# RWKV scan of a hybrid trunk: products laid straight or crossed over the array, value and key parts taken ahead

## The reference

```
def step(state, inp):
    r_t, w_t, k_t, v_t, kk_t, a_t = inp
    sa = jnp.einsum("bhvk,bhk->bhv", state, -kk_t)
    state = (state * w_t[:, :, None, :] + sa[..., None] * (kk_t * a_t)[:, :, None, :]
             + v_t[..., None] * k_t[:, :, None, :])
    return state, jnp.einsum("bhvk,bhk->bhv", state, r_t)
```

## Time and profile before

| what | us |
|---|---|
| median of three runs | 3495.32 |
| profiled execution | 3495.7 |
| its span | 3493.9 |
| span from 478.2 to 1190.0: scan of layer 0 | 711.8 |
| span from 2224.4 to 2930.5: scan of layer 1 | 706.1 |
| TensorE busy in these two | 697.72 and 694.95 |
| VectorE busy | 191.41 and 191.40 |
| ScalarE busy | 228.00 and 227.82 |
| GpSimd busy | 241.34 and 241.53 |

### The profile page before, as it was taken

How to read it: one execution, slowest core, us unless ns; L and a number is a source line. 1 busy time by engine, 2 the same in 40 slices (tenths; PEclk the granted TensorE clock), 3 DMA queues, 4 the chain that set the end, 5 groups by cost and what they waited for, 6 DMA issues and landing times. The chain is left out here.

```text
span 3493.9 us, 64355 instructions
## 1 busy us (share of the span) xinstructions
PE 3155.2 (90%) x24596; PEld 2315.9 (66%) x24596; DVE 1483.0 (42%) x2280; ACT 1145.7 (33%) x2332; POOL 961.4 (28%) x880
## 2 busy tenths in 40 slices
PE   6979979999999799959969799799999997999599
PEld 4768857777777544447747688577777775444477
DVE  4127722222222367567441277222222223675674
ACT  4004422333333245433240044223333333354332
POOL 4101011244343323332241010112444443233322
PEclk9989989999999879979989899899999998799699
DMA  3224532333333200077332245323333332000763
GB/s 125 73 74 146 165 88 80 96 101 107 104 105 106 81 25 28 6 210 214 117 119 73 76 144 165 91 82 98 101 105 107 107 103 75 25 28 6 214 211 116
DMA packets 408876, 357.82 MB, mean 102 GB/s; under 512 B 102792, under 2 KB 345992, under 8 KB 408584
## 3 DMA queue, kind: packets, MB, share of 16 engines
q1 hardware_dynamic: 339656, 312.93, 29.2%
q10 hardware_dynamic: 68928, 40.93, 4.3%
HBM read 222.97 MB, written 130.84 MB: 101 GB/s over the span
## 5 line engine op out<-in xcount | busy, mean ns | idle before, releaser
L124 PE MATMUL rs_acc<-h_hi,rs_w_hi 128*128 128x512 f32 x1024 | 425.4, 415 | 0.0
L128 PE MATMUL rs_acc<-h_lo,rs_w_hi 128*128 128x512 f32 x1024 | 415.5, 406 | 0.0
L130 PE MATMUL rs_acc<-h_hi,rs_w_lo 128*128 128x512 f32 x1024 | 412.0, 402 | 0.0
L124 PE MATMUL rp_acc<-h_hi,rp_w_hi 128*128 128x512 f32 x512 | 206.1, 402 | 40.9 <-PEq L121 40.9
L1466 ACT ACTIVATE fx_prob<-fx_ST 128x512 f32<-128x512 f32 (+3 forms) x320 | 157.8, 531 | 230.7 <-PE fx_ST L1328 123.3
L1752 PE MATMUL so_acc<-so_wo_hi,so_m_hi 128*128 128x512 f32 x512 | 210.2, 411 | 25.5 <-POOL so_m_lo L1674 21.4
L124 PEld LDWEIGHTS rs_acc<-h_hi,rs_w_hi 128*128 128x128 f32 x1024 | 192.1, 188 | 53.4 <-issue 16.5
L130 PEld LDWEIGHTS rs_acc<-h_hi,rs_w_lo 128*128 128x128 f32 x1024 | 192.5, 188 | 41.4
L128 PEld LDWEIGHTS rs_acc<-h_lo,rs_w_hi 128*128 128x128 f32 x1024 | 192.6, 188 | 35.6
L124 PE MATMUL pj_acc<-h_hi,pj_w_hi 128*128 128x512 f32 (+1 forms) x512 | 207.1, 404 | 5.2 <-PEq L121 5.2
L128 PE MATMUL rp_acc<-h_lo,rp_w_hi 128*128 128x512 f32 x512 | 208.0, 406 | 0.0
(11 more groups left out here) (257 smaller groups left out, 6496.0 us busy)
## 6 DMA issues: line engine op xcount, KB each, us to landing
projT<-rs_stage SPq DMA_DIRECT2D x128, 256.0 KB, 2.3
pj_xb<-x SPq DMA_DIRECT2D x32, 512.0 KB, 3.4
projT<-rp_stage SPq DMA_DIRECT2D x64, 256.0 KB, 3.1
rs_raw<-w_in ACTq DMA_DIRECT2D x32, 512.0 KB, 4.5
rs_nat<-rw SPq DMA_DIRECT2D x128, 128.0 KB, 2.4
so_stage<-x SPq DMA_DIRECT2D x64, 256.0 KB, 3.1
rp_pre<-projT SPq DMA_DIRECT2D x16, 899.5 KB, 7.5
projT<-pj_stage SPq DMA_DIRECT2D x56, 256.0 KB, 2.0
```

The lines of the kernel that those rows point to most:

```text
L124: ins = M(acc, self.w_hi[q][:, k, 0:m], self.h_hi[:, k, cols], start=(k == 0), stop=False)
L128: M(acc, self.w_hi[q][:, k, 0:m], self.h_lo[:, k, cols], start=False, stop=False)
L130: ins = M(acc, self.w_lo[q][:, k, 0:m], self.h_hi[:, k, cols], start=False, stop=(k == KC - 1))
```

## The change

Each product goes through `product`. For odd heads either its input or its output is crossed: chunk 0 of the head lies in partitions 64 to 127 and chunk 1 in 0 to 63. A straight input with a crossed output (or the reverse) makes the products of two neighbouring heads use the four quarters of the array; even heads write to one bank, odd heads to the next. s5 goes from straight to straight. The inputs of a tile are partly loaded crossed (`later`). N, b and k are formed in one group p1, with another copy of N by `beside`. Additions of the identity or of an earlier term that VectorE made become products with the identity (`unity`, `plus`). For both chunks the parts of the state step with wz and with vm are issued ahead of g; only the part with S stays in c0 and c1. SCAN_FILL is dealt out anew. norm_sum(t,3) goes from behind the filler of g to behind that of s9, `square(t, 3)` on ScalarE from behind wz into s8, and the wait for the factor of (t,3) from c1 to ahead of the products taken ahead. The units' sums go to `bk[:, 3, 256:512]`. The forget gates' steps come later on every engine. The core of the diff:

```diff
-SCAN_FILL = (("tok", 7), ("p2", 5), ("s3", 5), ("s4", 4), ("s5", 5), ("s6", 5), ("s7", 6), ("s8", 5), ("s9", 6), ("wz", 6), ("g", 8), ("c0", 10), ("c1", 22), ("y", 2))
+SCAN_FILL = (("p1", 5), ("p2", 6), ("s3", 5), ("s4", 5), ("s5", 5), ("s6", 5), ("s7", 5), ("s8", 5), ("s9", 5), ("wz", 6), ("g", 7), ("c0", 9), ("c1", 24), ("y", 4))
...
+        def pair(k, a, n=1):
+            return bk[:, 2 * k:2 * k + 2, :].rearrange("p e (i c) -> p i e c", i=2)[:, :, :, 64 * a:64 * (a + n)]
...
-                if i == 2:
+                if i == 3:
...
-                for n, buf, slot in ((0, cr[e], (0, 3)), (1, cr[e], (1, 2)), (2, bt, None), (3, kt, None)):
+                for n, buf in ((0, cr[e][:, :, 0, :]), (1, cr[e][:, :, 1, :]), (2, bt[:]), (3, kt[:])):
                     for c in two:
                         src = rw[n * GW:(n + 1) * GW, bass.ds(t * 128 + 64 * c, 64)].rearrange("(h c) t -> c h t", c=64)
-                        sp.dma_start(buf[half[c]] if slot is None else buf[half[c], :, slot[c], :], src).then_inc(i_in[e], 16)
-                for j, n in enumerate((0, 2, 3, 4)):
-                    sp.dma_start(nat[:, j], rw[n * GW:(n + 1) * GW, bass.ds(t * 128, 128)].rearrange("(k p) t -> p k t", p=128)).then_inc(i_in[e], 16)
+                        sp.dma_start(buf[half[c]], src).then_inc(i_in[e], 16)
+                sp.dma_start(nat[:, 0], rw[0:GW, bass.ds(t * 128, 128)].rearrange("(k p) t -> p k t", p=128)).then_inc(i_in[e], 16)
+                later = nat[:, 1:4].rearrange("p j k t -> p (j k) t")
+                src = rw[2 * GW:5 * GW, bass.ds(t * 128, 128)].rearrange("(n e c) t -> e c n t", e=2, c=64)
+                sp.dma_start(later[half[0]], src[0]).then_inc(i_in[e], 16)
+                for c in two:
+                    sp.dma_start(later[half[1], :, 64 * (1 - c):64 * (1 - c) + 64], src[1][:, :, 64 * c:64 * c + 64]).then_inc(i_in[e], 16)
...
                 gates_biased(t)
-                gates_log(t)
                 for i in range(4):
-                    if i == 1:
-                        gates_low(t)
                     if i == 1 and t + 1 < NT:
                         J.pool_weights(pool, (t + 1) % 2)
+                    if i == 2:
+                        gates_log(t)
                     if (t, i) in unit:
                         scale(unit[t, i])
+                gates_low(t)
...
-            def pairs(out, left, right):
-                for h in range(NH):
-                    for c in two:
-                        ins = M(out(h, c), left(h, c), right(h, c), start=True, stop=True)
+            def at(h, c, crossed):
+                return half[c ^ (h & 1) if crossed else c]
+            def out(k, a, n, h, p):
+                return bk[p, 2 * k + h % 2, 256 * (h // 2) + 64 * a:256 * (h // 2) + 64 * (a + n)]
+            def beside(p, h):
+                return bk[p, 2, 256 * (h // 2) + 128 + 64 * (h % 2):256 * (h // 2) + 192 + 64 * (h % 2)]
+            def some(i):
+                return [(2 * i + e, u) for e in two for u in two]
+            def product(k, a, n, left, right, crossed, to, plus=None):
+                for i in two:
+                    for h, c in some(i):
+                        p = at(h, c, crossed)
+                        ins = M(out(k, a, n, h, at(h, c, to)), left(p, h), right(p, h), start=True, stop=plus is None)
+                    if plus is not None:
+                        for h, c in some(i):
+                            p = at(h, c, crossed)
+                            ins = M(out(k, a + n - 1, 1, h, at(h, c, to)), eye[p], plus(p, h), start=False, stop=True)
                 return ins
-            def of(buf, *at):
-                return lambda h, c: buf[(half[c], h) + at]
-            def slots(buf, a, n=1, b=None):
-                b = a if b is None else b
-                return lambda h, c: buf[half[c], h, (a, b)[c]:(a, b)[c] + n, :] if n > 1 else buf[half[c], h, (a, b)[c], :]
-            E1, E2 = DE[:, 1], DE[:, 2]
+            def of(buf, a=None, n=1):
+                if a is None:
+                    return lambda p, h: buf[p, h, :]
+                return lambda p, h: buf[p, h, a, :] if n == 1 else buf[p, h, a:a + n, :]
+            def unity(p, h):
+                return eye[p]
+            straight, crossed = False, True
...
                 take(pe, i_in[e], 192)
-                pairs(of(bank(0)), slots(cr[e], 0, b=3), of(bt)).then_inc(s["n_rdy"], 1)
-                pairs(of(wide(1)), of(bt), slots(cr[e], 0, 2, b=2)).then_inc(s["mb"], 1)
-                pairs(of(wide(2)), of(kt), slots(cr[e], 0, 2, b=2)).then_inc(s["mk"], 1)
-                take(pe, s["y_ev"])
                 for j in range(4):
                     for p in two:
-                        ins = Tr(bk[:, 3 + j // 2, (2 * (j % 2) + p) * 128:(2 * (j % 2) + p + 1) * 128], nat[:, j, p, :], ident[:])
+                        ins = Tr(bk[:, 4 + j // 2, (2 * (j % 2) + p) * 128:(2 * (j % 2) + p + 1) * 128], nat[:, j, p, :], ident[:])
                 ins.then_inc(s["tok"], 1)
-                fill("tok")
+                take(pe, s["y_ev"])
+                product(0, 0, 1, of(cr[e], 0), of(bt), straight, crossed)
+                product(0, 1, 2, of(bt), of(cr[e], 0, 2), straight, crossed).then_inc(s["ab_m"], 1)
+                product(1, 0, 2, of(kt), of(cr[e], 0, 2), straight, crossed)
+                for h in range(NH):
+                    for p in two:
+                        ins = M(beside(half[p], h), cr[e][half[p], h, 0, :], bt[half[p], h, :], start=True, stop=True)
+                ins.then_inc(s["k_m"], 1)
+                fill("p1")
                 take(pe, s["d_rdy"])
-                pairs(of(bank(0)), slots(br, 1, b=2), of(DE[:, 0])).then_inc(s["p2_m"], 1)
-                pairs(of(bank(1)), of(DE[:, 0]), slots(br, 1, b=2)).then_inc(s["p2t_m"], 1)
+                take(pe, s["tok_ev"])
+                product(2, 0, 1, of(br, 1), of(br, 0), crossed, straight).then_inc(s["p2_m"], 1)
+                product(0, 0, 1, of(br, 0), of(br, 1), crossed, straight)
+                product(0, 1, 1, of(br, 0), unity, crossed, straight).then_inc(s["px_m"], 1)
                 fill("p2")
+                take(pe, s["p2_a"])
+                take(pe, s["px_d"])
+                product(2, 0, 1, of(px, 0), of(p2), straight, crossed).then_inc(s["s3a"], 1)
+                product(0, 0, 2, of(p2), of(px, 0, 2), straight, crossed, plus=of(px, 1)).then_inc(s["s3d"], 1)
+                fill("s3")
+                take(pe, s["k_rdy"])
                 norm_sum(t, 0)
-                take(pe, s["p2_a"])
-                take(pe, s["p2_d"])
-                pairs(of(bank(0)), slots(px, 0), of(p2)).then_inc(s["s3a"], 1)
-                pairs(of(wide(1)), of(p2), of(px)).then_inc(s["s3d"], 1)
-                fill("s3")
                 take(pe, s["p4_a"])
                 take(pe, s["x2_d"])
-                pairs(of(bank(1)), of(p4), of(x1)).then_inc(s["s4d"], 1)
-                pairs(of(bank(0)), of(p4t), of(p4)).then_inc(s["s4a"], 1)
-                take(pe, s["tok_ev"])
-                take(pe, s["ak_rdy"])
-                pairs(of(bank(3)), slots(kr, 1, b=2), of(vm)).then_inc(s["q_m"], 1)
+                product(0, 0, 1, of(p4), of(q4, 1), crossed, straight, plus=of(q4, 1)).then_inc(s["s4d"], 1)
+                product(2, 1, 1, of(kr, 0), of(vm), crossed, straight)
+                product(2, 0, 1, of(q4, 0), of(p4), crossed, straight).then_inc(s["s4a"], 1)
                 fill("s4")
                 take(pe, s["p8_a"])
                 take(pe, s["x3_d"])
-                pairs(of(bank(1)), of(p8), of(x1)).then_inc(s["s5"], 1)
+                product(0, 0, 1, of(p8), of(x1), straight, straight).then_inc(s["s5"], 1)
                 fill("s5")
                 norm_sum(t, 1)
-                for xr, sa, sd, xa, yd, E, sx, f1, f2 in (("x4", "s6a", "s6d", "x4_a", "y_d", E1, "s7", "s6", "s7"), ("x5", "s8a", "s8d", "x5_a", "y2_d", E2, "s9", "s8", "s9")):
+                for k, xr, sa, sd, xa, yd, sx, f1, f2 in ((0, "x4", "s6a", "s6d", "x4_a", "y_d", "s7", "s6", "s7"), (1, "x5", "s8a", "s8d", "x5_a", "y2_d", "s9", "s8", "s9")):
                     take(pe, s[xr])
-                    pairs(of(bank(1)), of(E), of(x1)).then_inc(s[sd], 1)
-                    pairs(of(bank(0)), of(x1), lambda h, c: eye[half[c], :]).then_inc(s[sa], 1)
+                    product(0, 0, 1, of(E[:, k]), of(x1), straight, crossed).then_inc(s[sd], 1)
+                    if k == 0:
+                        take(pe, s["q_a"])
+                    product(2, 0, 1, of(x1), unity, straight, crossed).then_inc(s[sa], 1)
                     fill(f1)
                     take(pe, s[xa])
                     take(pe, s[yd])
-                    pairs(of(bank(2)), of(xn), of(yy)).then_inc(s[sx], 1)
+                    product(0, 0, 1, of(xn), of(yy), crossed, straight).then_inc(s[sx], 1)
                     fill(f2)
-                    if f2 == "s7":
-                        norm_sum(t, 2)
```

(73 more changed lines are left out.)

131 lines of the change are left out of this document (56 added, 75 removed).

## The result

The changed kernel takes 3505.84 us (median of 14 runs), the kernel before 3496.09 (median of 14 on the same chip): 1.0035 times as long, 95% interval 1.0025 to 1.0046. The profiled execution took 3504.48 us, its span 3502.7. One of the 14 runs of the changed kernel took 3981.67 us, at a granted clock of 0.72 where the others have 0.91 to 0.92; the ratio and its interval leave it out and are not the quotient of the two medians.

A forecast was written before the change was run, and what follows sets the result against it. TensorE was taken to bound the recurrence stage. Tiles with two units gain 31 us, 22 with four lose 42, last tiles and starts add 2 each: +15, forecast 3510 us, own range 3485 to 3540, full range 3430 to 3575.

The forecast's parts named there:

- z in the tile: Start of the first accumulator's evacuation, counted from the tile's start: 15.29 us before, 13.6 predicted with faster products.
- wait for the factor ahead of g: TensorE waits for unit (t,3)'s factor before the products taken ahead: 1.1 us in all 32 tiles (0.6 to 1.6).
- wait ahead of (t,3): TensorE reaches norm_sum(t,3) at z+9.9, before its late-loaded unit is ready: a wait of 4.3 us.
- slow clock, on top: Stretch at the lower clock behind the long wait, in four of five tiles: 1.1 us on average, between 0 and 2.8.
- four-unit tile: Tile with four normalisation units beside it: 45.4 us against a mean of 44.6, plus 1.1 for the clock.
- starts and last tiles: Start of the stages +2 us; last tile of each layer, without GpSimd's weights, +1 each.
- The price of four quarters: A product round on four array quarters costs what two do: blocks go from 0.87 to 0.44 and 0.47 to 0.235 us.
- Rival 2: Four quarters bring nothing for products on 64 columns: +117 us, 3626 us; chance 0.08.
- Rival 1: The wait for unit (t,3) is absent or short because SP's chain runs sooner: 134 us gained, 3362 us; chance 0.15.
- SP's twelve loads ... cost at nothing, they have a whole tile: SP's loads of the next tile stay twelve and cost nothing; if that failed, some 0.3 us.
- nothing of SP's order is changed in it: Argument against rival 1: the chain feeding unit (t,3) hangs on z, with SP's order unchanged; norm_sum at z+14.25.
- Rival 3: The clock falls twice a tile, after either long wait: 2.8 us instead of 1.1, +41 us, 3551 us; chance 0.12.

The follow-up runs named there:

- e10: e6 with crossing taken out, so all products of 64 rows use the two diagonal quarters (pairing of odd heads wrong): 3508.27 us, 190 us more than e6.
- e1: The changed kernel with four buffers for the units' inputs instead of two, loaded four units ahead: 3355.49 us, ratio 0.9606 to the kernel before.
- e3: The kernel before with only norm_sum(t,3) moved behind the filler of s9 and its Square into s8: 3605.56 us, ratio 1.0327.
- e11: The changed kernel with norm_sum(t,3), its Square and factor again behind g, the sum in bank 1: 3453.49 us, ratio 0.9881 to the kernel before.
- e14: e7 with the next tile's weights on GpSimd moved behind the scaling of (t,1): 3459.49 us, ratio 0.9889 to the kernel before.
- e7: The changed kernel with the forget gates' stores and load back behind unit 2 in SP's order: 3520.00 us, ratio 1.0080 to the kernel before.
- e6: e1 with factor(t,3) ahead of the evacuation in stage wz on ScalarE: 3317.81 us, ratio 0.9490 to the kernel before.

## Why the prediction came out right

| term | predicted | measured |
|---|---|---|
| z in the tile | 13.6 | 13.60 |
| two-unit tile | 38.9 | 38.8 |
| 8 of them | -31 | -28.3 |
| wait for the factor ahead of g | 1.1 | 0.99 (32 times, 31.6 in all) |
| norm_sum(t,2) | z+5.65, wait 1.1 | z+8.31, wait mostly 3 to 4 |
| norm_sum(t,3) | z+14.25 (13.8 to 15.0) | z+15.36 |
| wait ahead of (t,3) | 4.3 | 0 to 1.8 |
| from it to the end | 17.55 | 17.53 |
| slow clock, on top | 1.1 | 0.2, within the z+15.36 (in tile 10 1.7 us, all inside the wait) |
| four-unit tile | 46.5 | 46.49 |
| 22 of them | +42 | +41.6 |
| starts and last tiles | +4 | -4.3 |
| sum | +15 | +9.0 in the scans |

**Products.** The price of four quarters was right for both widths (e10). By the page of the Trainium skill that the prediction quoted ("TensorE: Matmul & The Clock Gate", "Wait — 56ns, not 53.3ns?") 16 records on 64 columns would take 0.40 us. The trace has 0.23 (952.11 to 952.34), 15 ns a record, so across different quarters the trace disagrees. Rival 2 is out.

**The wait that takes the gain.** Its mechanism is shown from three sides: away with it and the gain is there (e1), the move alone costs 111 us (e3), undoing the move gives back 52 (e11, 40 of it in the four-unit tiles). The chain that feeds (t,3) is as rows 4 to 6 were read (e14). Rival 1 needed norm_sum(t,3) at z+9.9 and is out.

**Two terms were mis-sized and cancel.** norm_sum(t,3) started at z+15.36 and not at z+14.25, outside the 13.8 to 15.0 given for it: 1.1 us a tile. Over the 22 tiles its Square starts at z+14.69, no sooner than in the kernel before (z+14.66). The forecast had taken z+14.35 from two tiles, which was 0.3 too early for the mean, and had given back 0.57 for the removed f_hi step. GpSimd's weights do start 0.43 sooner (z+2.11 instead of z+2.54), but from the load of qx to that of cs SP takes 2.87 us instead of 2.27, so the cs load is issued at z+11.52, before at z+11.33; what holds SP there was not traced (2.31 in e7, 2.99 in e14). In 7 of the 22 tiles TensorE comes to (t,3) later than the Square allows, 0.2 us a tile on average over all 22.

That 0.2 is all that the slow clock cost on top in these tiles: norm_sum(t,2) to TensorE's arrival at (t,3) took 5.9 us in tile 10 (940.05 to 945.95, that is 947.66 less its wait) against 4.2 in e6, but TensorE then waited for (t,3) anyway. Had I sized only one of the two rightly, the forecast would have moved by some 20 to 24 us, up or down. That 3510 lies so near to 3505.84 is in part luck. (Two of the forecast's sums are loose without effect: 8.7 and 1.1 make 9.8 and not 9.9, and the stretch to the end adds up to 17.53.)

**The step that failed** is "SP's twelve loads ... cost at nothing, they have a whole tile", and with it "nothing of SP's order is changed in it". The units keep their order among themselves, but what SP waits for moved: SCAN_FILL completes accumulation 2 so late that unit 3 comes to the edge of the tile and the gates behind it fall into the next one, where they hold up the twelve loads. That took the wait to unit (t,2), from the 1.1 us predicted to mostly 3 to 4, and left (t,3) less than 2. The gates' place behind unit 3, a line of the diff whose effect in SP's queue I did not price, is part of it: on e11's base putting it back was worth 82 us, while on the changed kernel itself it cost 14.

**The clock.** Rival 3, two falls a tile, is not what happened: in 21 of 22 tiles it fell once, in or behind the first wait. My term of 1.1 us took a fall to cost the same wherever it stands; it costs something only as far as no later wait covers it (e7).

## What to carry to other kernels

When a bound engine gets faster, list every buffer that is refilled at its old pace, and compute the time at which each is ready from the chain that feeds it; the first one that is late takes the gain, and a second buffer may be worth more than the faster instruction. Moving work between stages moves the completion of whatever the stages complete, so follow each store to its place in the DMA queue, also over the edge of the loop. A wait has two prices, its length and the slow clock behind it, and the second is paid only if no other wait follows close.
